# The two later normalisations of a two-block transformer kernel, by token halves

## The reference

```python
def first_block(x, c, ...):                       # one layer
    mod = silu(c) @ w_ada + b_ada                 # sh1, sc1, gt1, sh2, sc2, gt2
    u = modulate(rmsnorm(x, g_mix), sh1, sc1)
    h = x + gt1 * hybrid_mixer(u, ...)            # attention + S5; its last step is merged @ w_out
    u = modulate(rmsnorm(h, g_ffn), sh2, sc2)     # the second normalisation
    h = h + gt2 * conv_ffn(u, w_up, w_conv, b_conv, w_down)
    return rmsnorm(h, g_final)                    # feeds the second block

def hybrid_layer_2(x, ...):                       # the second block
    h = rmsnorm(x, norm_g)                        # the third normalisation, on the result of rmsnorm above
    p = h @ w_in                                  # u, v, z_a, x_b, b_g, c_g, z_b, x_c, z_c, g_a, g_b, g_c
    ...                                           # gated branches a, b, c
    return x + merged @ w_o                       # and a last rmsnorm
```

## Time and profile before

| | us |
|---|---|
| three runs, median (lowest, highest) | 2208.72 (2208.28, 2209.03) |
| the profiled execution, its own time | 2206.25 |
| its span | 2204.5 |
| PE busy in the span | 2144.0 (97%) |
| DVE, ACT, POOL busy | 780.8, 410.9, 1049.5 |

### The profile page before, as it was taken

One profiled execution on the slowest core, in us unless ns is written; L12 is line 12 of the kernel. 1 busy time (PEld: TensorE's weight loads), 2 busy tenths in 40 slices (PEclk: granted clock), 3 DMA queues, 4 the chain that ended last, 5 costly groups with the idle time before them and its releaser, 6 DMA issues.

```text
span 2204.5 us, 25383 instructions
## 1 busy us (share of the span) xinstructions
PE 2144.0 (97%) x10478; PEld 1784.7 (81%) x10478; DVE 780.8 (35%) x1009; ACT 410.9 (19%) x548; POOL 1049.5 (48%) x451
## 2 busy tenths in 40 slices
PE   7999999999999899999999889999999999999997
PEld 3788888888887788888888788888888888888886
DVE  6961355555642521222222654310022111231232
ACT  3202233323311310201111321110000110110202
POOL 1548347563464345445363705435545355535550
PEclk9999999999999899999999989999999999999999
DMA  9545554544441002011120321012111011101131
GB/s 346 125 103 153 182 163 143 160 139 152 154 171 57 29 20 86 20 56 48 40 64 29 96 96 58 30 38 67 46 50 48 29 57 57 48 29 57 38 124 76
DMA packets 157105, 192.08 MB, mean 87 GB/s; under 512 B 11152, under 2 KB 138720, under 8 KB 157024
## 3 DMA queue, kind: packets, MB, share of 16 engines
q1 hardware_dynamic: 148096, 172.05, 25.1%
q10 hardware_dynamic: 8928, 18.88, 2.3%
HBM read 159.20 MB, written 31.70 MB: 87 GB/s over the span
## 4 chain that ended last, share of the span: by engine, by line
PE 94%; DVE 2%; POOL 1%; DMA 1%; SPq 1%; ACT 0%; issue 0%; DVEq 0%; POOLq 0%; ACTq 0%
PE ps L713 62%; PE ps L735 10%; PE ps L787 8%; PE ps L745 4%; PE ps L1010 3%; PE ps L971 2%; PE ps L985 1%; PE ps L903 1%; POOL w_h L634 1%; PE ps L881 1%; PE ps L1154 1%; DMA ada_w<-in_w_ada 1%; POOL w_l L636 1%; PE ps L874 0%; DVE nrm L1672 0%; DVE act_l L1683 0%
## 5 line engine op out<-in xcount | busy, mean ns | idle before, releaser
L634 POOL TENSOR_SCALAR w_h<-raw 128x1024 fp32r<-128x1024 f32 (+2 forms) x202 | 508.0, 2515 | 941.9 <-PE ps L713 593.1
L713 PE MATMUL ps<-act_h,w_h 128*128 128x512 f32 x1536 | 598.9, 390 | 1.7 <-POOL w_l L636 1.3
L713 PE MATMUL ps<-act_l,w_h 128*128 128x512 f32 x1536 | 597.6, 389 | 0.0
L713 PE MATMUL ps<-act_h,w_l 128*128 128x512 f32 x1536 | 597.6, 389 | 0.0
L636 POOL TENSOR_TENSOR w_l<-raw,w_h 128x1024 fp32r<-128x1024 f32 (+2 forms) x202 | 437.2, 2164 | 16.8
L713 PEld LDWEIGHTS ps<-act_h,w_h 128*128 128x128 f32 x1536 | 288.3, 188 | 64.1 <-issue 2.4
L713 PEld LDWEIGHTS ps<-act_h,w_l 128*128 128x128 f32 x1536 | 288.3, 188 | 60.2
L713 PEld LDWEIGHTS ps<-act_l,w_h 128*128 128x128 f32 x1536 | 288.4, 188 | 59.5
L713 PE MATMUL ps<-in_h,w_h 128*128 128x512 f32 x384 | 149.4, 389 | 0.0
L713 PE MATMUL ps<-in_l,w_h 128*128 128x512 f32 x384 | 149.4, 389 | 0.0
L713 PE MATMUL ps<-in_h,w_l 128*128 128x512 f32 x384 | 149.4, 389 | 0.0
(11 more groups left out here) (312 smaller groups left out, 2788.6 us busy)
## 6 DMA issues: line engine op xcount, KB each, us to landing
raw<-in_w_in SPq DMA_DIRECT2D x45, 1024.0 KB, 5.3
raw<-in_w_up SPq DMA_DIRECT2D x16, 1024.0 KB, 5.5
ada_w<-in_w_ada SPq DMA_DIRECT2D x8, 1024.0 KB, 11.9
ada_lo<-in_w_ada SPq DMA_DIRECT2D x16, 512.0 KB, 3.9
ada_hi<-in_w_ada SPq DMA_DIRECT2D x16, 512.0 KB, 4.4
gates_scratch<-gate_st ACTq DMA_DIRECT2D x32, 256.0 KB, 2.3
gate_in<-gates_scratch SPq DMA_DIRECT2D x16, 512.0 KB, 4.5
raw<-in_w_down SPq DMA_DIRECT2D x16, 512.0 KB, 3.5
```

What stands on the lines that cost most here:

```text
L634: nc.gpsimd.tensor_scalar(w_h[:, k, c, :], src[:, c, :], 1.0, None, ALU.mult).then_inc(s["w_high"], 1)
L713: last = nc.tensor.matmul(dst[:, tok], w[:, k, kw + c, P * cg:P * cg + P], x[:, c, tok], start=(c == 0 and p == 0), stop=(c == kc - 1 and ...
```

## The change

All that is said of "half" is half of the tokens: th = 0 is tokens 0 to 511, th = 1 tokens 512 to 1023.

- Output projection: the loop is written out. Chunks 0 to 3 are as before. Chunks 4 to 7 are computed for th = 0, then for th = 1. `statistics` of th = 0 (4 matmuls) stands in PE's list behind chunk 4 of th = 1, `everywhere` of th = 0 behind chunk 5 of th = 1.
- FFN: the first pair of chunks and the next two are computed for th = 0 and then for th = 1 in the first quarter (`pair_half`). `statistics` of th = 1 stands within the first pair, `everywhere` of th = 1 behind it. Quarters 0 and 3 are written out, 1 and 2 stay in a loop.
- Last down projection: chunks 6 and 7 by halves, with both statistics of th = 0 between chunk 6 and chunk 7 of th = 1, and two `everywhere` behind them.
- Product `v`: the token tiles of th = 0 first (slots 0 and 2), then those of th = 1 (slots 1 and 3). The first can start when half of the split of its second weight block is there. Both statistics of th = 1 stand behind input chunk 5, two `everywhere` further on.
- DVE and ACT do the residual, the squares, their sums, the roots, the diagonals and the scale/high/low steps in matching halves of 512 tokens. The scale of the third normalisation reads its factor from PSUM; only the other factor is copied out. The first normalisation keeps its whole width.
- POOL's split of N_A waits for three of the four slots of `v`. SP's load of `ws_tok` moves behind the loads of N_A and N_A+1 and waits for the last `everywhere`, since `diag_a` lies where `ws_tok` goes. GELU reads the slots in the order 0, 2, 1, 3.

The diff, cut to its core:

```diff
-                pe.wait_ge(s["out_read"], 4 * i + (AHEAD - 2))
-                product_pair((0, 1), 1, KD, act_h, act_l, s["merged_ready"])
...
-            statistics(acc, KD - 1, slot(3))
-            everywhere(2, slot(3), 0)
+            for th in range(2):
+                for u in range(4):
+                    if th == 0:
+                        split_done(N_OUT + 2 + u // 2)
+                        pe.wait_ge(s["out_read"], AHEAD + u + 1)
+                    product_half(slot(u), 1 - u // 2, u % 2, KD, act_h, act_l, th)\
+                        .then_inc(s["gemm"] if th else s["first_half"], 1)
+                    if th and u == 0:
+                        statistics(acc, 7, slot(0)[:, 0:4], 0)
+                    if th and u == 1:
+                        everywhere(2, slot(3)[:, 0:HALF], diag_a[:, 0]).then_inc(s["rstd_ready"], 1)
...
+            split_done(N_FFN)
+            pair_half((0, 1), 1, 0, U_FFN, lambda: statistics(acc, 11, slot(2)[:, HALF:HALF + 4], 1))
+            everywhere(3, slot(3)[:, HALF:T], diag_a[:, 1]).then_inc(s["rstd_ready"], 1)
+            split_done(N_FFN + 1)
+            for cg in range(2):
+                product_half(slot(2 + cg), 0, cg, KD, act_h, act_l, 0)
+            pair_half((0, 1), 1, 1, U_FFN + KD)
+            for cg in range(2):
+                product_half(slot(2 + cg), 0, cg, KD, act_h, act_l, 1).then_inc(s["gemm"], 1)
...
+            for th in range(2):
+                for u in (6, 7):
...
+                    product_half(slot(u % 4), 0, u % 2, 4, in2_h, in2_l, th).then_inc(s["gemm"] if th else s["first_half"], 1)
+                    if th and u == 6:
+                        for m in range(2):
+                            statistics(acc2[:, m, :], 24 + m, slot(0)[:, HALF * m:HALF * m + 4], 0)
+            everywhere(4, slot(1)[:, HALF:T], diag_b[:, 0]).then_inc(s["rstd_ready"], 1)
+            everywhere(5, slot(1)[:, 0:HALF], diag_b[:, 1]).then_inc(s["rstd_ready"], 1)
...
+                for b in range(2):
+                    if c == 0:
+                        pe.wait_ge(s["w_half"], N_V2 + b + 1)
+                    if c == KD // 2:
+                        split_done(N_V2 + b)
+                pe.wait_ge(s["u_ready"], U_IN2 + c + 1)
...
+                if c == 5:
+                    second_sums()
```

ACT and DVE, around the second and around the third normalisation:

```diff
+            for c in range(4, KD):
+                residual(c, 0)
+                add_square(c - 1, 0 if c > 4 else None)
+            add_square(7, 0)
+            residual(4, 1)
+            one_over_root(2, slice(0, 4))
+            on_diagonal(diag_a[:, 0], stat[:, 1, 0:4])
+            residual(5, 1)
+            add_square(4, 1)
             dve.wait_ge(s["rstd_ready"], 2)
+            norm(U_FFN, slice(0, HALF), lambda i: nrm[:, i, 0:HALF], gain[:, 1], shift_ffn, slot(3)[:, 0:HALF], second_half)
+            residual(7, 1)
+            add_square(6, 1)
+            add_square(7, 1)
...
+            residual2(6, 0)
+            add_squares(5)
+            residual2(7, 0)
+            add_squares(6, 0)
+            add_squares(7, 0)
+            residual2(6, 1)
+            both_norms(0, 4, 4, slot(0)[:, HALF:HALF + 4], diag_b)
+            dve.wait_ge(s["rstd_ready"], 5)
+            norm(U_IN2, slice(0, HALF), lambda i: sq[:, i, 0:HALF], gain2, None, slot(1)[:, 0:HALF], last_half)
+            both_norms(1, 6, 6, slot(3)[:, HALF:HALF + 4], diag_a)
+            scaled_out(0)
+            dve.wait_ge(s["rstd_ready"], 7)
+            norm(U_IN2 + KD, slice(HALF, T), lambda i: sq[:, i, HALF:T], gain2, None, slot(3)[:, 0:HALF])
+            scaled_out(1)
```

More of the change, by code:

```diff
@@ L684, in _ @@
             pairs(N_V2, 1)
-            single(N_A)
+            split(N_A, N_A % 2, 16 * (N_A // 2 + 1), units_before(N_V2) + 3)
             single(N_A + 1)
@@ L1100, in _, with down, at_q @@
+            def down(i, off, end):
+                def at_q(m, k):
+                    return k + m * off if i is None else i * m + (k + m * off)
+                pe.wait_ge(s["a_read"], at_q(4, 4))
+                split_done(at_q(8, N_FFN + 4))
+                product_pair((0, 1), 1, 4, in2_h, in2_l, s["f_ready"], at_q(4, AHEAD))
+                for u in range(2, end):
                     if u % 2 == 0:
-                        split_done(8 * q + N_FFN + 4 + u // 2)
+                        split_done(at_q(8, N_FFN + 4 + u // 2))
@@ new lines, in _ @@
+            for b in range(2):
+                for t in (1, 3):
+                    for c in range(KD):
+                        last = rows_chunk(slot(2 * b), 1 - b, 0, t, c)
+                    if b == 0 and t == 1:
+                        everywhere(6, slot(3)[:, HALF:T], diag_a[:, 0]).then_inc(s["rstd_ready"], 1)
+                        everywhere(7, slot(3)[:, 0:HALF], diag_a[:, 1]).then_inc(s["rstd_ready"], 1)
+                last.then_inc(s["gemm"], 1)
+            pe.wait_ge(s["rstd1_read"], 1)
@@ new lines, in _ @@
+            for c in range(KD):
+                pe.wait_ge(s["u_ready"], U_IN2 + KD + c + 1)
+                for t in (0, 2):
+                    rows_chunk(slot(1), 1, 4, t, c)
+            for t in (1, 3):
+                for c in range(KD):
+                    last = rows_chunk(slot(1), 1, 4, t, c)
+            last.then_inc(s["gemm"], 1)
+            pe.wait_ge(s["rstd1_read"], 2)
+            for t in range(4):
+                for c in range(KD):
+                    last = rows_chunk(slot(3), 0, 4, t, c)
@@ new lines, in keep_rstd @@
+            def keep_rstd(th, ready, src):
+                act.wait_ge(s["rstd_ready"], ready)
+                A.activation(rstd1[:, HALF * th:HALF * th + HALF], src, ACT.Copy).then_inc(s["rstd1_read"], 1)
+            for c in range(KD - 2):
+                squares(c)
+            for th in range(2):
+                squares(KD - 2, th)
+                if th == 0:
+                    squares(KD - 1, 0)
+            roots(0, 3, slot(0)[:, 0:4])
+            keep_rstd(0, 4, slot(1)[:, HALF:T])
@@ L1970, in quarter @@
                          .then_inc(s["f_ready"], 1)
-                for u in range(KD):
+                for u in range(KD - 2 if last else KD):
                     dve.wait_ge(s["gemm"], 16 * q + base_f + 8 + u + 1)
```

350 lines of the change are left out of this document (205 added, 145 removed).

## The result

| | before | changed |
|---|---|---|
| median of 6 runs each (lowest, highest), us | 2208.43 (2206.41, 2209.03) | 2198.82 (2197.52, 2201.06) |
| the profiled execution, its span | 2206.25, 2204.5 | 2197.53, 2195.8 |
| output projection, from its first matmul to the first matmul of the last down quarter (stretch A) | 586.12 | 578.65 |
| from there to the end of `v`, the first matmul of block N_A (stretch B) | 119.55 | 116.20 |
| ahead of A | 626.09 | 628.14 |

The ratio is 0.9959 [0.9947, 0.9972]: 9.6 us faster, where 22.8 were forecast, and 2.8 us above the upper end of the range. The direction held, the size is less than half. The stretches are differences of start times in the trace.

A forecast was written before the change was run, and what follows sets the result against it. PE, busy 97% of the span, bounds the kernel; only its standstills and slow clock can be won. Gains 14.0 (A) + 8.8 (B) = 22.8 us take the profiled 2206.25 to 2183.5; with the median 2.5 higher, 2186, range 2177.5 to 2196.

The forecast's parts named there:

- The end of the output projection: Second normalisation: th = 0 halves ready in time, so PE goes on into the FFN without the 16.9 us standstill.
- The th = 1 sum is ready at 5.6, PE asks at 6.8.: Second normalisation, us after the output projection's end: DVE's sum of squares comes before PE needs it, so no wait.
- 14.0 forecast: Net gain in A: loss of 19.9 us, less 3.9 for statistics and spreads, less 2.0 for weights.
- The gain of under 10 us: Sign named beforehand: a gain in A under 10 us would prove the timing of the halves wrong.
- Port, "3.0 us": B: DVE instructions with two SBUF inputs slowed beside POOL's split; 16 at 0.19 us each, ends 0 and 11.7.
- The second rival: Port rules: each of 16 DVE instructions waits half a POOL instruction, 1.4 us; 22 us instead of 3, 2205; chance 0.10.
- The weights, 2.0: A: PE may wait for POOL's weight splits beside half chunk products; 2.0 us lost, ends 0 and 4.
- The third normalisation, 9.0 + 3.7: B: 9.0 us from the down products to `v` instead of 27.0, then a 3.7 us wait for input chunk 4.
- B = 76.0 before: Old kernel's time from the end of the down products to the end of `v`, the base for B's gain of 8.8.
- The clock, 1.5: B: PE's remaining short waits may lower its clock; 1.5 us lost, ends 0 and 5.
- Rival 5: Clock never comes back, `v` runs at 1.2 GHz: all 384 matmuls cost 34.6 us, 2219; chance 0.03.
- Moves, 0: Moved `ws_tok` load, x2 stores, GELU and POOL's N_A split stay hidden around and behind `v`; cost 0.

The follow-up runs named there:

- one input: Changed kernel, but POOL writes `w_l` of four weight blocks (FFN's first two, both of `v`) as raw times zero, omitting their low part; 2184.58 us, ratio 0.9895.
- low in PSUM: Changed kernel with the scaled values of th = 0 at the second and third normalisation written to free PSUM halves instead of SBUF; 2188.81 us, ratio 0.9915.
- squares in PSUM: The three together, plus third-normalisation squares of chunk 5 and of chunks 6 and 7 (th = 0) written to PSUM; 2182.52 us, ratio 0.9888.
- the three together: Changed kernel with low in PSUM, the 128x8 product ahead of the FFN, and sum later; 2185.31 us, ratio 0.9902.
- sum later: Changed kernel with PE's second-normalisation `statistics` of th = 1 behind the first FFN pair, its `everywhere` behind the next half chunk; 2192.04 us, ratio 0.9929.

## Why the prediction was wrong

- **The end of the output projection.** Held. FFN follows without a wait. The halves of th = 0 were in time in every kernel.
- **"The th = 1 sum is ready at 5.6, PE asks at 6.8."** Failed. PE asked at 7.0, the sum was there at 12.9. This is the step that broke in A, and it had no port term at all: the prediction charged the port to the third normalisation only, though POOL splits FFN weights right beside the input chunks of the second. Three low parts and the sum carry 2.0 + 1.4 + 1.4 + 2.0 = 6.8 us of waiting for `w_l`. With the cause taken away or made small A gains 14.7 (one input) and 14.6 us (low in PSUM) against the 14.0 forecast, and 15.9 where no wait is left. The gain of under 10 us that was to prove the timing of the halves wrong came (7.5), yet the timing as such was right: 15.9 is close to the 19.9 - 3.9 = 16.0 of the forecast.
- **Port, "3.0 us", ends 0 and 11.7.** The term of B that was mis-sized. In the changed kernel the chain pays 2.2 for the 128x8 product, 1.5 for one half sum, and 2.0 and 1.4 for two low parts, 7.1 in all, and the waits carry a slow clock with them. Against the one-input kernel the whole of B is 6.1 us longer. I took the median of 14 sums and stayed near it. A median over instructions says nothing when only 30 of the 198 instructions with two SBUF inputs meet the thing and pay four fifths of it. The second rival had the mechanism, and its sign, sums and low parts of over 1 us at 512 elements, is what the trace shows; but it had 1.4 us for each of all 16, which is too much, since only those that start within `w_l` pay for the rest of it. It went to 22 us and a chance of 0.10, where both the mechanism and the count were to be had from the order of time.
- **The rule on the port.** The Trainium skill's "SBUF — State Buffer", section "Who interferes with whom", has a vector instruction with two SBUF inputs contend with a GpSimd instruction that reads SBUF, and the later one wait for the whole of the other. The trace agrees for `w_l` (29 of 30 lengthened). For `w_h`, which reads SBUF with one input, it agrees only for the first 0.9 us: those that began later in a `w_h` of 2.77 us took their usual time. The measurement decides.
- **The weights, 2.0.** Nothing. PE's only waits for the `w_l` of a product in the whole trace after, 1.1 and 0.6 us, lie outside A and B, at 2085 and 86 us. That the 14.0 of A was met by 14.7 and 14.6 thus hides this term of 2.0 behind a wait of 0.8 to 1.0 us that the prediction did not have. Once the low parts were fast, PE did wait for weights, in a place that the prediction did not name: 2.3 to 4.2 us ahead of `v`.
- **The third normalisation, 9.0 + 3.7.** 16.8 us from the prediction's zero (1250.49 in the trace after) to the first of `v` at 1267.31, where 10.5 were to be seen: 5.2 instead of 1.4 for the sum, 3.57 instead of 2.0 for the statistics and 4.75 instead of 2.7 for the last product, both mostly at the lower clock, and 4.4 instead of 2.5 for the first low part, against 0 instead of 1.2 for the diagonals. Within `v` the wait was 2.9 instead of 3.7. "End of `v` 67" was 72.7. With one input it was 66.6, and with the squares in PSUM 61.7, with the first matmul of `v` at 8.8. The sum's wait of 1.4 was small by its own prices as well: the operations listed for it add up to 6.6 us from -7.3, which is -0.7 and not -1.3, and the 128x8 product is not among them. (At the second normalisation, the eighth input chunk at 3.4 is 3.9 by the pace given; nothing hangs on it.)
- **Statistics and spreads within `v`, 2.0 + 1.9.** 1.68 and 1.72. **`v` itself**: 264 matmuls in 31.67, as forecast.
- **B = 76.0 before.** The stretch was read right, but it holds a slow clock of 3.7 us that the same code did not have in the profile of the kernel with only the second normalisation changed.
- **The clock, 1.5.** Too small: in B 9, 15 and 14 matmuls behind three waits ran at half pace, 1.9 + 1.5 + 1.4 = 4.8 us beside the slow statistics, near the upper end of 5. In A, where the slower clock was to go, there were 7, for 1.5 us. Much of it hangs on the longer waits, but not all: the wait of 2.9 us was shorter than forecast and had it too. Rival 5 failed: `v` had 29 slow matmuls and ran the other 355 at full clock.
- **Moves, 0.** Held: 872.7 to 873.1 us behind `v` in all ten profiles.

## What to carry to other kernels

Before pricing DVE work that will run beside GpSimd, list the DVE instructions by the GpSimd instruction in which they begin, and compare durations between those groups; a median over all hides a cost that few pay in full. A scratch value that DVE will read together with a second SBUF operand belongs in PSUM where a slot is free: that alone gave 10 of the 13 us that were missing here. Where PE asks for a result that DVE makes under such waits, move the asking instruction behind the next independent product before anything is made faster: 5.9 us here.

## What the runs showed of the hardware that I had not expected

- A DVE instruction of 128x8 elements took 2.36 us instead of 0.16, as long as the rest of POOL's `w_l`, and with it gone the next one took the wait over.
- Beside POOL's one-input instruction the wait is there too, but ends about 0.9 us into it: +0.85 us at 0.04, +0.31 at 0.58, 0 from 0.97 on.
- Beside a `w_l`, 20 (before) and 21 (changed) DVE instructions with one PSUM input took no longer at all. The other way round POOL's `w_h` took 3.21 to 3.76 instead of 2.77 us where it began beside a DVE instruction with two SBUF inputs, as at 1234.61 in the three together.
- One input instead of two in POOL's instruction cut the waits from up to 2.0 us to at most 0.9 at 512 elements, though the instruction grew from 2.8 to 3.15 us.
- The granted clock fell to its lower level behind PE's waits of 6.0, 5.2, 4.4 and 2.9 us (changed kernel), 2.3 (squares in PSUM) and 1.9 (sum later), and stayed up behind 0.8 (one input), 1.0 (low in PSUM) and 1.4 (squares in PSUM). Behind one of 3.4 ahead of `v`, with the same code there, it was low in one execution and high in another, so the length of the wait alone does not decide it.
